# Two-block sequence kernel: 256-column products in three passes against a 512-column and a 256-column product, in the output and feed-forward projections

## The reference

```python
        merged = jax.nn.sigmoid(g_s5) * br_s5 + jax.nn.sigmoid(g_dn) * br_dn
        x = x + jnp.einsum("bld,de->ble", merged, w_out[l])
        h = rmsnorm(x, ffn_norm_w[l])
        up = causal_dwconv(jnp.einsum("bld,df->blf", h, ffn_up[l]), ffn_conv_w[l])
        act, val = jnp.split(up, 2, axis=-1)
        x = x + jnp.einsum("blf,fd->bld", jax.nn.silu(act) * val, ffn_down[l])
...
def swiglu(h, w1, w3, w2):
    return (jax.nn.silu(h @ w1) * (h @ w3)) @ w2
```

## Time and profile before

| | us |
|---|---|
| three runs | 3741.64, 3743.77, 3745.2 (median 3743.77) |
| span of the profiled execution, first to last instruction | 3733.5 |
| median of the runs less that span | 10.3 |
| PE busy | 3530.5 (95%) |
| PEld busy | 3226.8 (86%) |
| DVE busy | 2252.3 (60%) |
| ACT busy | 1692.3 (45%) |

### The profile page before, as it was taken

One profiled execution on the slowest core, in us unless ns is written; L12 is line 12 of the kernel. 1 busy time (PEld: TensorE's weight loads), 2 busy tenths in 40 slices (PEclk: granted clock), 3 DMA queues, 4 the chain that ended last, 5 costly groups with the idle time before them and its releaser, 6 DMA issues. The chain is left out here.

```text
span 3733.5 us, 83474 instructions
## 1 busy us (share of the span) xinstructions
PE 3530.5 (95%) x33402; PEld 3226.8 (86%) x33402; DVE 2252.3 (60%) x3904; ACT 1692.3 (45%) x2572; POOL 110.0 (3%) x159
## 2 busy tenths in 40 slices
PE   9999998998999999999899997888888899999998
PEld 8998887777899999999788965776677899999998
DVE  5758885665577777556643553676675644444444
ACT  5547773323455555444312434444443455555333
POOL 0000000000000000000000001211110000000000
PEclk9999999998999999999999998999998999999999
DMA  5547765444455555555322464000003455555553
GB/s 199 180 145 276 258 249 189 154 165 141 168 171 185 184 180 180 192 186 183 114 100 91 158 226 157 6 7 7 7 6 114 156 181 181 182 185 179 176 177 133
DMA packets 83117, 572.09 MB, mean 153 GB/s; under 512 B 9585, under 2 KB 11889, under 8 KB 18129
## 3 DMA queue, kind: packets, MB, share of 16 engines
q1 hardware_dynamic: 81216, 560.60, 43.2%
q0 software_dynamic: 1680, 8.36, 0.6%
HBM read 566.82 MB, written 2.10 MB: 152 GB/s over the span
## 5 line engine op out<-in xcount | busy, mean ns | idle before, releaser
L251 DVE TENSOR_TENSOR w_lo<-raw,w_hi 128x1024 fp32r<-128x1024 f32 x880 | 1038.8, 1200 | 398.5 <-ACT w_hi L244 394.2
L244 ACT ACTIVATE w_hi<-raw 128x1024 fp32r<-128x1024 f32 (+1 forms) x877 | 897.5, 1037 | 666.8 <-PE po L267 422.2
L265 PE MATMUL po<-hh,w_lo 128*128 128x256 f32 x3744 | 1065.2, 285 | 18.5 <-DVE hh L361 9.0
L266 PE MATMUL po<-hh,w_hi 128*128 128x256 f32 x3744 | 1060.9, 283 | 0.0
L267 PE MATMUL po<-hh,w_hi 128*128 128x256 f32 x3744 | 1060.7, 283 | 0.0
L265 PEld LDWEIGHTS po<-hh,w_lo 128*128 128x128 f32 x3744 | 720.0, 192 | 25.7 <-issue 23.3
L266 PEld LDWEIGHTS po<-hh,w_hi 128*128 128x128 f32 x3744 | 720.3, 192 | 0.3
L267 PEld LDWEIGHTS po<-hh,w_hi 128*128 128x128 f32 x3744 | 720.1, 192 | 0.0
L265 PE MATMUL po<-f_hi,w_lo 128*128 128x256 f32 x1408 | 400.7, 285 | 6.1 <-DVE f_lo L1776 6.1
L267 PE MATMUL po<-f_hi,w_hi 128*128 128x256 f32 x1408 | 400.2, 284 | 0.0
L266 PE MATMUL po<-f_lo,w_hi 128*128 128x256 f32 x1408 | 400.1, 284 | 0.0
(11 more groups left out here) (579 smaller groups left out, 6191.0 us busy)
## 6 DMA issues: line engine op xcount, KB each, us to landing
raw<-ffn_up SPq DMA_DIRECT2D x176, 1024.0 KB, 4.9
raw<-w_in SPq DMA_DIRECT2D x112, 1024.0 KB, 5.0
raw<-ada SPq DMA_DIRECT2D x86, 1024.0 KB, 6.4
raw<-ffn_down SPq DMA_DIRECT2D x64, 1024.0 KB, 4.9
raw<-w_out SPq DMA_DIRECT2D x32, 1024.0 KB, 4.9
raw<-ffn_down SPq DMA_DIRECT2D x32, 768.0 KB, 4.2
raw<-glu SPq DMA_DIRECT2D x16, 1024.0 KB, 6.4
ada_third<-ada SPq DMA_DIRECT2D x10, 1024.0 KB, 6.8
```

The lines of the kernel that those rows point to most:

```text
L244: act.activation(w_hi[:, k % 4, 0:width], raw[:, k // 2 % ring, (k % 2) * PW:(k % 2) * PW + width], ACT.Copy).then_inc(hi_ready, 1)
L251: dve.tensor_tensor(w_lo[:, k % 4, 0:width], raw[:, k // 2 % ring, (k % 2) * PW:(k % 2) * PW + width], w_hi[:, k % 4, 0:width].bitcast(F32 ...
L265: pe.matmul(po[bank][:, 0:T], lo, act_hi[:, t, :], start=first and n == 0, stop=False)
L266: pe.matmul(po[bank][:, 0:T], hi, act_lo[:, t, :], start=False, stop=False)
```

## The change

In `w_out`, `w_out2`, `ffn_up`, `ffn_up2`, `ffn_down` and `ffn_down2`, the two parts of the activation are put in one tensor (`h_pair`, `mg`, `om`, `ff`), so that one matmul can stream both: for each weight tile `wide_products` issues one matmul of 512 columns (`w_hi` by both parts, into both halves of the bank) and one of 256 columns (`w_lo` by the rounded part, into the first half). The sum over the three products is then spread over both halves of the bank, and the eviction adds them: `sum_halves` with a `tensor_reduce` over a stride of 256, `add_halves` and `add_gated_halves` with two instructions, the second waiting for the first. In `ffn_up`, the bank is first reduced to a tile in SBUF (`f_sum`, in the place where `f_lo` of that tile will lie), the convolution reads that tile, and that of tile a is done in the body of the next piece (k = 2 and 6). Silu moves from k = 1 to k = 2 on ACT. In `ffn_up2`, tile a is reduced into `conv_a` and Silu works there, tile v into `f_sum`. The other projections are unchanged.

```diff
+        def wide_products(pe, rnd, k, tiles, bank, pair, first, last, turn=None, split=None):
+            if turn is not None:
+                pe.wait_ge(free[bank], turn)
+            pe.wait_ge(lo_ready, rnd * 8 + k + 1)
+            for n, (s, t) in enumerate(tiles):
...
+                pe.matmul(halves(bank), hi, pair[:, :, t, :], start=first and n == 0, stop=False)
+                mm = pe.matmul(po[bank][:, 0:T], lo, pair[:, 0, t, :], start=False, stop=last and n == len(tiles) - 1)
...
+        def sum_halves(dve, out, bank):
+
+            settle(dve)
+            return dve.tensor_reduce(out, po[bank][:].rearrange("p (s t) -> p t s", s=2), AX.X, ALU.add)
+
+        def add_halves(dve, xt, o, phase, i):
+
+            dve.tensor_tensor(xt, po[o][:, T:2 * T], xt, ALU.add).then_inc(half_added, 1)
+            dve.wait_ge(half_added, i * 4 + (HALF0[phase] + o + 1))
+            dve.tensor_tensor(xt, po[o][:, 0:T], xt, ALU.add).then_inc(free[o], 1)
...
         def ffn_up_act(act, phase, f, round_act):
             def body(i, rnd, k):
                 j = i * 2 + k // 4
-                if k % 4 == 1 and f == 0:
-                    act.wait_ge(*freed(phase, i, 4, k // 2))
+                if k % 4 == 2:
+
+                    act.wait_ge(ff_conv, j + (KF * f + 1))
+                    settle(act)
                     act.activation(conv_a[:], conv_a[:], ACT.Silu).then_inc(ff_silu, 1)
-                if k % 4 == 1 and f == 1:
-                    act.wait_ge(used, rnd * 8 + k + 1)
-                    act.wait_ge(ff_prod, j + KF)
-                    act.activation(conv_a[:], po[k // 2][:, 0:T], ACT.Silu).then_inc(free[k // 2], 1)
...
-                if k % 4 == 1 and f == 0:
+                total = f_sum[:, ds(j, 1), :].rearrange("p a t -> p (a t)")
+                if k % 4 == 1:
                     dve.wait_ge(used, rnd * 8 + k + 1)
-                    conv(dve, conv_a[:], o, w, 3, at).then_inc(free[o], 1)
+                    if f == 0:
+                        sum_halves(dve, total, o).then_inc(free[o], 1)
+                    else:
+                        sum_halves(dve, conv_a[:], o).then_inc(free[o], 1)
+                        dve.wait_ge(*freed(phase, i, 4, o))
+                        dve.sem_inc(ff_conv, 1)
+                if k % 4 == 2 and f == 0:
+                    dve.wait_ge(*freed(phase, i, 4, o - 1))
+                    w_a = lambda n: par[:, ds(i * 4 + (COL["ffn_conv"] + 88 * n + o - 1), 1)]
+                    conv(dve, conv_a[:], total, w_a, 3, i * 8 + (CONV0 + 2 * (o - 1))).then_inc(ff_conv, 1)
                 if k % 4 == 3:
                     dve.wait_ge(used, rnd * 8 + k + 1)
...
+                    sum_halves(dve, total, o).then_inc(free[o], 1)
+                    dve.wait_ge(*freed(phase, i, 4, o))
+                    if f == 0:
+                        conv(dve, conv_v[:], total, w, 3, i * 8 + (CONV0 + 2 * o)).then_inc(conv_v_done, 1)
+                        dve.wait_ge(conv_v_done, j + 1)
+                    dve.wait_ge(ff_silu, j + (KF * f + 1))
+                    dve.tensor_tensor(conv_v[:], conv_v[:] if f == 0 else total, conv_a[:], ALU.mult).then_inc(ff_prod, 1)
...
-                        dve.tensor_tensor(x[:, n, :], po[o][:, 0:T], x[:, n, :], ALU.add).then_inc(free[o], 1)
+                        add_halves(dve, x[:, n, :], o, "ffn_down", i)
```

More of the change, by code:

```diff
@@ L268, in products, with halves, project_wide @@
             return mm
+        def halves(bank):
+            return po[bank][:].rearrange("p (s t) -> p s t", s=2)
+        def wide_products(pe, rnd, k, tiles, bank, pair, first, last, turn=None, split=None):
[3 more added lines that the diff above has]
+            for n, (s, t) in enumerate(tiles):
+                if split is not None and n % 4 == 0:
+                    pe.wait_ge(*sv.at(split, f"lo{t // 4}"))
+                hi = w_hi[:, k % 4, s * P:s * P + P]
+                lo = w_lo[:, k % 4, s * P:s * P + P]
+                pe.matmul(halves(bank), hi, pair[:, :, t, :], start=first and n == 0, stop=False)
+                mm = pe.matmul(po[bank][:, 0:T], lo, pair[:, 0, t, :], start=False, stop=last and n == len(tiles) - 1)
+            return mm
+        def project_wide(pe, phase, rounds, pair, split=None):
+            with pe.Fori(0, rounds) as i:
+                rnd = i + ROUND0[phase]
+                for k in range(8):
+                    o, half = k // 2, k % 2
+                    turn = i + TURN0[phase] if half == 0 else None
+                    wide_products(pe, rnd, k, [(s, half * 8 + s) for s in range(8)], o, pair,
+                                  half == 0, half == 1, turn, split if k < 2 else None).then_inc(used, 1)
         def project(pe, phase, rounds, act_hi, act_lo, k_tiles, r_off=0, t_off=0, split=None):
@@ L290, in project_down @@
                     tiles = [(t, s * 8 + t) for t in range(8 if s < 5 else 4)]
[L291 to L292 removed]
+                    wide_products(pe, rnd, k, tiles, o, ff, s == 0, s == 5,
+                                  i + TURN0[phase] if s == 0 else None).then_inc(used, 1)
         def down_width(q):
@@ L452, in program, with add_gated_halves @@
         conv_sum = sem("conv_sum")
+        half_added, ff_conv, conv_v_done = sem("half_added"), sem("ff_conv"), sem("conv_v_done")
+        HALF0 = {"w_out": 0, "ffn_down": 16, "w_out2": 32, "ffn_down2": 48}
         CONV0 = 72
         ff_silu, ff_prod, ff_hi, ff_lo = sem("ff_silu"), sem("ff_prod"), sem("ff_hi"), sem("ff_lo")
+        def sum_halves(dve, out, bank):
[5 more added lines that the diff above has]
+            dve.tensor_tensor(xt, po[o][:, 0:T], xt, ALU.add).then_inc(free[o], 1)
+        def add_gated_halves(dve, xt, o, gate, phase, i):
+            dve.scalar_tensor_tensor(xt, po[o][:, T:2 * T], gate, xt, ALU.mult, ALU.add).then_inc(half_added, 1)
+            dve.wait_ge(half_added, i * 4 + (HALF0[phase] + o + 1))
+            dve.scalar_tensor_tensor(xt, po[o][:, 0:T], gate, xt, ALU.mult, ALU.add).then_inc(free[o], 1)
         def bc4(ap):
```

55 lines of the change are left out of this document (21 added, 34 removed).

## The result

The changed kernel takes 3718.39 us, median of five runs (3706.73 to 3729.63), against 3741.64 for the kernel before in the same comparison (3741.3 to 3745.2): ratio 0.9937, interval 0.9924 to 0.9951. It is 23 us faster. 3701 was forecast, with 3684 to 3716: the time lies 2.4 us above the range, and about half of the forecast gain is missing. The five runs also spread by 23 us, where the five of before spread by 4. A part of the spread goes with TensorE's granted clock: in one comparison the fastest and the slowest run of the kernel before had mean clocks of 0.973 and 0.967 (3729.03 and 3745.36 us), and the changed kernel's fastest and slowest had 0.972 and 0.967.

What follows compares the result with a forecast made beforehand. PE was taken to bound the changed phases, with DVE loops taking over in ffn_up. Terms -44.3 - 3.3 + 0.6 + 4.0 = -43.0 us, from 3743.8 to 3701 us; range 3684 to 3716.

Steps and rivals of the forecast that it cites:

- the first term: Six changed phases: a set falls 13.3 ns to 346.7; 44.3 us over 3328 sets without the first block's ffn_up.
- two bounds: PE's gain per set: none, if 512 columns cost like two products (240 ns), or 13.3 ns, which was taken.
- DVE's loop with the table load: ffn_up: DVE's own work of 10.85 us a pair, 11.47 in every second pair with a 0.62 us wait for w_hi.
- The loop through PE: ffn_up: DVE's chain from reduction to w_lo, then PE's sets, takes 11.42 us a pair, longer than PE's 11.09.
- PE's waits: ffn_up: PE waits for w_lo once in a pair, 0.3 to 0.4 us each, some 15 us in all.
- The reduction: DVE in ffn_up: summing 512 elements from PSUM to 256 results takes 0.69 us, bounded by 0.43 and 1.75.
- TENSOR_SCALAR from SBUF: ffn_up: the convolution's first instruction, reading f_sum, takes near 0.36 us in place of 0.48.
- The ends of phases: PE drains at the six phase ends, so DVE's longer eviction is exposed there: 4.0 us lost.
- ACT's later Silu: ffn_up, every second pair: Silu ends 1.28 + 0.42 us after tile a's convolution, hidden with 1.9 us to spare.
- PE stays the bound in ffn_up too: Rival: with a reduction nearer 0.43 us, ffn_up gains 15.8 to 18.8 us; time 3685 to 3689; chance 0.22.
- The fixed cost does not go: Rival: the wide product costs as two, 3753 us, or a set gains only 2.5 ns, 3742 us; chance 0.05.
- The formula of the page: TensorE skill page: a warm product takes N/2.4 + 2.5 ns, so a set gains only 2.5 ns; 3742 us in all.

Runs made afterwards that it cites:

- evictions of before: Changed kernel with ffn_up's reductions removed and its earlier evictions restored, leaving out one of three products there: 3698.74 us, ratio 0.989.
- w_lo wanted later: Changed kernel with products in groups of eight, four or two, PE waiting for w_lo only ahead of the 256-column products: 3705.92, 3703.47, 3700.07 us.
- the early w_lo: Changed kernel with DVE making w_lo of piece k+3 right behind tile v's reduction in ffn_up, ahead of its convolution: 3746.87 us, ratio 1.0025.

## Why the prediction was wrong

**The step that failed** is the first term: "A set becomes 226.7 + 120 = 346.7 ns". Each width was measured among products of its own width, and the prediction said that no row shows the two alternating; its lower bound was no gain at all, but the range did not use the room between. A set measured 346.7 or 353.3 ns; in the second case half of the 13.3 ns is gone. In the five phases without ffn_up this cost 13.4 us in the first profile (w_out, ffn_up2 and half of ffn_down slow: 256, 1408 and some 350 sets x 6.67 ns), and 16.4 in the second. The prediction gave the six phases 47.0 us (44.3 and 3.3, less 0.6), and the profiles show 27.8 on the mean: of the 19.2 missing, 14.9 are these sets and 3.9 are ffn_up. The profile of before could not give the number, but the prediction's own two bounds could have given a wider range: halfway between no gain and 13.3 ns lies 6.7 ns a set, and over 3328 sets this is 22 us.

**ffn_up** was right in its mechanism and off by 3.9 us: 3.3 of gain were forecast, and on the mean of two profiles it took 0.6 more than before. DVE's loop with the table load was 11.47 in the sum and 11.48 in the trace. The loop through PE was 11.42 and measured 11.52 at the fast level: 5.41 from the reduction to w_lo's end (5.40), PE starts 0.05 later (0.15), its 16 sets need 5.54 with the restart (5.43), and DVE starts 0.52 after the last product's start (0.44). At the slow level it is 11.62. Mean 11.50 to 11.55, where 11.52 was before. PE's waits were forecast at some 15 us. In the trace the starts in ffn_up that come late, waits and restarts, add up to 18.0 us. Of these 2.7 are the phase's start, which the kernel before has too; the others come once in a pair. Without the loop (evictions of before, or w_lo wanted later) ffn_up dropped to 491 to 499.

**Prices.** The reduction: 0.69 forecast, 688 and 692 ns measured. TENSOR_SCALAR from SBUF: 0.36, and 354 and 348 ns. The ends of phases: 4.0 forecast, 3.5 measured (the 0.31 behind ffn_down counted up to w_in2's end). ACT's later Silu cost nothing, as forecast, in the changed order, but the same ACT chain made the early w_lo fail.

**Rivals.** "PE stays the bound in ffn_up too" fell with the 0.69. "The fixed cost does not go" was half true in an unforeseen way: in a fast stretch it goes, in a slow one half of it stays. The formula of the page "TensorE: Matmul & The Clock Gate" in the Trainium skill, section "Back-to-back issue gap", which the page gives for an isolated product, would have a set gain 2.5 ns; 6.7 and 13.3 are measured, so the trace disagrees again.

**The frame.** The prediction took the changed kernel's other parts as unchanged. The issue stalls at one line rose by some 4 us. The middle part took 1052.9 to 1065.6 us in twelve profiles with wide products (mean 1058.7) and 1051.6 and 1055.1 in the two of before. The difference is not the clock's alone: the two wide profiles under 1055 us had 105 and 106 us at 1.2 GHz, where the two of before had 118.6 and 129.0. What makes the rest of it isn't known. The forecast also started from a median of 3743.77 us, and the kernel before took 3741.64 in the comparison, which hid 2 us of the miss.

**Open:** what in PE sets the level, at a pause or at a break in the order, and why ffn_up2 began slow in each of the six profiles of kernels with one wide and one narrow product in turn.

## What to carry to other kernels

A duration taken from a steady stream of one shape is not that shape's duration in a mixed stream: leave some ns a product for the mixing, and try products in groups of two. When two loops bound a stretch nearly alike, look for the consumer that can want the late operand later; here one wait moved by two products was worth more than the whole of ffn_up's edit. Before an instruction is moved up, ask what the producer it waits for is itself queued behind.

## What the hardware showed that was not expected

- Products of 512 and 256 columns in turn, with new weights for each, take 346.7 or 353.3 ns a set, constant for up to 1394 sets. After a pause of PE the level was the other one in 65 of 125 cases. Streams of only 256 (120 ns) or only 512 columns (226.7 ns) showed one level.
- The level also changes without a pause: with the narrow product first and one break in the order for each output, the outputs of ffn_down2 ran at 353.3 and 346.6 ns in turn, 15 in a row.
- Groups of two, four and eight products of one width showed one level each: 348.3, 350.8 and 349.2 ns a set in ffn_up2.
- After a change from 256 to 512 columns the first five products took 228 to 236 ns and the later ones 226.7.
- A pause of 0.22 us cost PE 0.10 us more: the first set after it took 0.45 us, and 0.45 to 0.46 after each of the 43 pauses of that phase.
